# Sums over partitions as two half-width matmuls: diagonal quarters for the head sums, column halves for the sums over all features

## The reference, cut to what matters

```python
def rms_norm(x, gain):
    xf = x.astype(jnp.float32)
    y = xf * lax.rsqrt(jnp.mean(xf * xf, axis=-1, keepdims=True) + EPS)
    return (y * gain.astype(jnp.float32)).astype(x.dtype)
...
h = rms_norm(x, norm_mix[i])                # over all 1024 features, twice a layer
q = rms_norm(qkv[:, :, 0], q_gain)          # over the 64 features of each head
k = rms_norm(qkv[:, :, 1], k_gain)
```

## Time and profile before

| | |
|---|---|
| median of 3 runs | 2962.67 us (2961.53 to 2964.29) |
| the profiled execution | 2964.98 us |
| its span | 2962.8 us |
| TensorE busy (matmuls) | 2815.3 us, 95% of the span |
| TensorE weight loads (beside the matmuls) | 2238.2 us, 76% |
| GpSimd, ACT, DVE busy | 46%, 37%, 34% |
| mean granted TensorE clock | 0.983 |

### The profile page before, as it was taken

One profiled execution on the slowest core, in us unless ns is written; L12 is line 12 of the kernel. 1 busy time (PEld: TensorE's weight loads), 2 busy tenths in 40 slices (PEclk: granted clock), 3 DMA queues, 4 the chain that ended last, 5 costly groups with the idle time before them and its releaser, 6 DMA issues.

```text
span 2962.8 us, 35778 instructions
## 1 busy us (share of the span) xinstructions
PE 2815.3 (95%) x13900; PEld 2238.2 (76%) x13900; DVE 1014.8 (34%) x1906; ACT 1100.3 (37%) x1644; POOL 1370.1 (46%) x1073
## 2 busy tenths in 40 slices
PE   7899899999989999998899998999999899899999
PEld 5876678888756788887677776788887866678887
DVE  3034431113476411225465554311122034431112
ACT  4245442223445422333333433422334245443222
POOL 3466644445464444444243342444445366444443
PEclk9999999999989999999999999999999999999999
DMA  4232123332431232333111110233322232123322
GB/s 120 85 80 57 43 72 100 99 99 85 100 71 44 66 99 92 99 99 93 29 43 43 29 43 29 72 100 100 99 94 84 86 71 60 34 85 100 99 91 79
DMA packets 271749, 227.70 MB, mean 77 GB/s; under 512 B 30100, under 2 KB 259220, under 8 KB 271620
## 3 DMA queue, kind: packets, MB, share of 16 engines
q1 hardware_dynamic: 260880, 216.29, 24.1%
q10 hardware_dynamic: 10740, 9.65, 1.4%
HBM read 223.61 MB, written 2.30 MB: 76 GB/s over the span
## 4 chain that ended last, share of the span: by engine, by line
PE 83%; DVE 7%; POOL 4%; ACT 4%; issue 1%; DMA 0%; ACTq 0%; DVEq 0%; POOLq 0%
PE bank L1756 47%; PE bank L1667 15%; PE bank L1815 5%; POOL w_lo L555 3%; PE bank L2125 2%; PE bank L2137 2%; PE bank L2134 1%; PE bank L1792 1%; PE bank L1710 1%; ACT w_hi L688 1%; POOL arena L577 1%; PE bank L1866 1%; PE bank L1970 1%; PE bank L1998 1%; PE bank L1882 1%
## 5 line engine op out<-in xcount | busy, mean ns | idle before, releaser
L555 POOL TENSOR_TENSOR w_lo<-raw,w_hi 128x512 fp32r<-128x512 f32 x808 | 1068.5, 1355 | 1268.3 <-ACT w_hi L688 1268.3
L688 ACT ACTIVATE w_hi<-raw 128x2048 fp32r<-128x2048 f32 x202 | 385.5, 1908 | 476.6 <-PE bank L1756 423.3
L1756 PE MATMUL bank<-h_hi,w_hi 128*128 128x512 f32 x1024 | 400.8, 391 | 0.0
L1756 PE MATMUL bank<-h_hi,w_lo 128*128 128x512 f32 x1024 | 398.4, 389 | 0.0
L1756 PE MATMUL bank<-h_lo,w_hi 128*128 128x512 f32 x1024 | 398.4, 389 | 0.0
L1756 PE MATMUL bank<-g_hi,w_hi 128*128 128x512 f32 x1024 | 398.3, 389 | 0.0
L1756 PE MATMUL bank<-g_lo,w_hi 128*128 128x512 f32 x1024 | 398.3, 389 | 0.0
L1756 PE MATMUL bank<-g_hi,w_lo 128*128 128x512 f32 x1024 | 398.3, 389 | 0.0
L1667 PE MATMUL bank<-h_hi,w_hi 128*128 128x512 f32 x784 | 331.0, 422 | 6.9 <-POOL w_lo L555 4.6
L1667 PE MATMUL bank<-h_lo,w_hi 128*128 128x512 f32 x784 | 321.1, 410 | 0.0
L1667 PE MATMUL bank<-h_hi,w_lo 128*128 128x512 f32 x784 | 317.9, 406 | 0.0
(11 more groups left out here) (261 smaller groups left out, 3932.7 us busy)
## 6 DMA issues: line engine op xcount, KB each, us to landing
raw<-in_mlp_w SPq DMA_DIRECT2D x128, 1024.0 KB, 5.2
raw<-in_a_w_in SPq DMA_DIRECT2D x48, 512.0 KB, 5.0
raw<-in_c_w_in SPq DMA_DIRECT2D x32, 512.0 KB, 5.2
raw<-in_a_w_in SPq DMA_DIRECT2D x12, 1024.0 KB, 5.0
raw<-in_b_w_in SPq DMA_DIRECT2D x18, 256.0 KB, 4.1
raw<-in_a_w_out SPq DMA_DIRECT2D x4, 1024.0 KB, 4.8
raw<-in_b_w_in SPq DMA_DIRECT2D x4, 1024.0 KB, 5.4
arena<-bias_scratch ACTq DMA_DIRECT2D x16, 256.0 KB, 3.5
```

The costliest lines, as they stand in the source:

```text
L555: ins = nc.gpsimd.tensor_tensor(w_lo[s][:, k, :], raw[s][:, k, :], w_hi[s][:, k, :].bitcast(F32), ALU.subtract)
L688: nc.scalar.activation(w_hi[s][:], raw[s][:], ACT.Copy).then_inc(w_hi_done, 1)
L1756: mm = nc.tensor.matmul(lin_bank[j][:], w[s][:, c, P * j:P * j + P], a[:, c, :], start=c + z == 0, stop=c == CT - 1 and z == 2)
```

## The change

Each of the three sums becomes two matmuls. For sums over all features (`norm`, `square_sum`) the first uses the left 64 columns of `ones` and writes partitions 0 to 63 of the bank, the second the right 64 columns and partitions 64 to 127; both contract over all 128 rows. For the head sums (`sum_qk`) the first uses rows 0 to 63 and columns 0 to 63 of `halves` on partitions 0 to 63 of the squares, the second rows and columns 64 to 127 on the other half, and the zero quarters of `halves` are not used. Where a semaphore is raised it is raised by the second matmul. The waits and everything else stay.

```diff
             def norm(m, columns=False):
 
                 pe.wait_ge(ss_added, ss_before(m) + 7)
-                mm = nc.tensor.matmul(stat_bank[:], ones, ss, start=True, stop=True)
+                for z in (0, HD):
+                    mm = nc.tensor.matmul(stat_bank[z:z + HD, :], ones[:, z:z + HD], ss, start=True, stop=True)
...
             def square_sum(m, c):
 
                 pe.wait_ge(sq_done, 8 * m + c + 1)
-                mm = nc.tensor.matmul(stat_bank[:], ones, sq[c % 2], start=c == 0, stop=c == CT - 1)
+                for z in (0, HD):
+                    mm = nc.tensor.matmul(stat_bank[z:z + HD, :], ones[:, z:z + HD], sq[c % 2], start=c == 0,
+                                          stop=c == CT - 1)
                 mm.then_inc(sq_summed if c < CT - 1 else norm_sum, 1)
...
                 sqs = mem[kind]["sq"]
-                nc.tensor.matmul(stat_bank[:], halves, sqs[Q % len(sqs)], start=True, stop=True).then_inc(ssq_done, 1)
+                for z in (0, HD):
+                    r = slice(z, z + HD)
+                    mm = nc.tensor.matmul(stat_bank[r, :], halves[r, r], sqs[Q % len(sqs)][r, :], start=True, stop=True)
+                mm.then_inc(ssq_done, 1)
```

## The result

The changed kernel takes 2981.4 us (median of 6 runs, 2975.37 to 2987.14) against 2964.44 us (6 runs) of the kernel before: a ratio of 1.0053 with a 95% interval of 1.0042 to 1.0063. It is slower by half a per cent, the forecast's sign and size: 15.7 us, where the ratio gives 15.7 us (12.5 to 18.7). Its profiled execution has a span of 2980.8 us, 18.0 more than the one before.

The account below looks back on a forecast made before the run. TensorE's stream, busy 95% and carrying 83% of the chain, was taken as the bound. Head sums 9.9, squares 3.6 and norms 2.2 us make 15.7, giving 2978.4 us on the median (2980.7 on the profiled execution); range 2968 to 2997.

Parts of the forecast that it names:

- The cost of a visit: Mid-stream on TensorE: 1.32 us from last product to second one after a sum becomes 0.32 + 1.02 + 0.34 = 1.68, +0.36.
- Side by side: Head sums' two diagonal quarters overlap as halves do, leaving only the cost of going in and out; chance 0.70, 2973 to 2986.
- The first rival: Head sums' quarters run in turn: 3012.8 us fully, 2995.6 if only first and last record stand alone; chance 0.13.
- How many are paid: On the chain: 40 of 58 head sums, 6 norms, 10 single squares and 2 pairs; 18 head sums and 2 squares covered.
- The second and third rival: Second, nearly free: head sums add nothing, 2968.5 us, chance 0.11. Third, faster: four records in one record time, 2953.5, chance 0.06.
- a sum behind a wait: Where TensorE waited for the squares: 1.19 us becomes 1.36, +0.17, for 9 head sums and 4 squares.
- Product on both sides: Sums between products on TensorE: 1.32 us becomes 1.68, +0.36, for 19 of the 40 head sums.

Follow-up runs that it names:

- lone quarter: Changed kernel with one layer 0 head sum given only its first quarter: 1.00 us for that quarter, as for a pair; no whole-kernel time is given.
- the head sums alone: Kernel before with only the 58 head sums divided into quarters, sums over all features left whole: 2973.77 us, ratio 1.0032.
- the float32r kernel: Kernel before with the 48 head sums of the two dilated-attention layers as one float32r matmul each: 2942.77 us, ratio 0.9934.

## Why the prediction was right

**The cost of a visit.** The steps 0.32, 1.02 and 0.34 came out as 0.32, 1.00 and 0.34. They were taken from other instructions (row halves of 384 and 512 columns, column halves of 128). Both new forms, 64x64 and 128x64, have the same steps. Between 1.02, taken from a form with 64 columns of weights, and 1.06, from row halves with 128, the former was the right one, so form is not quite without effect.

**Side by side.** The step with the most at stake, 34 us, rested on analogy, as the trace had no quarter. The lone quarter shows it directly. The first rival fell with it. The rule of the Trainium skill that was weighed against the rows (TensorEngine Tiling (Array Packing), Restrictions and Gotchas) says that different row tiles can't access the same PSUM bank at the same time; here they do, in different partitions of bank 7, at 1.00 us for two as for one. The measurement decides for this form; row tiles that write the same partitions were not run.

**How many are paid.** 40 head sums were put on the chain; in the changed kernel 42 of them are pieces of it, with 6 norms, 12 single sums of squares and the 2 pairs. Both squares of layer 0 that were covered before came in, and one head sum more in each attention layer, such as the one at 239.97. These four were not in the sum and may be worth up to 1.4 us. Doubling sums at paid and covered places confirmed the split: 0.87 us each against none.

**The second and third rival.** Covered sums are free, but GpSimd does not set the pace of the attention layers as a whole: the head sums alone cost 9.5 us. No quarter visit was under 1.32 us, and a record of a quarter takes as long as one of the whole array, so nothing could be gained.

**What the sum left out.** The steps sum to 15.6, and the profiled execution grew by 18.0. One term was mis-sized: that a sum behind a wait costs 0.17. At four of the nine such places (60.68, 73.69, 2270.16 and 2283.17 us before) the visit cost nothing. At the first of them, the time from the last product ahead of the sum to the second one behind it was 1.69 us (60.18 to 61.87) and is 1.66 now (61.68 to 63.34). The sum alone grew by 0.15 as forecast, but the division of the sum before had put the products later, and the squares were there when they ended. That is 0.7 us less than forecast. Product on both sides cost 0.34 instead of 0.36, 0.4 us less in all, and the four sums that came in make up to 1.4 us more.

Of the 18.0 us, 3.5 lie in the stretch of layer 2 where the granted clock stayed low for longer. That the ratio gives 15.7 as well is therefore in part luck. Its interval is 12.5 to 18.7, errors of either sign met in the sum, and both profiled executions of the changed kernel have the long stretch, which was not forecast. The six runs spread from 2975 to 2987 us; how much of that is layer 2 is not known, as only profiled executions show it.

## What to carry to other kernels

Price a divided matmul by the distance between its neighbours' starts, not by its own duration: in TensorE's stream of products dividing the array cost 0.34 us each time it was entered and left, with quarters as with column halves, and about 0.15 where divided work followed or where something only waited for the result. A wait ahead of it can swallow it whole. It gives something back only if the parts do different work that the whole array would do one after the other, as the row halves of the earlier trace rows do, four records in the time of two. Keep visits of the same form together, and look first at the number of passes: a sum against ones in full fp32 cost nearly four products, and a float32r one cost one. To say which copies of a repeated instruction matter, walk the chain and count them, then confirm with a doubled instruction at the places on it and off it. And before a difference of a few microseconds is explained, compare how long the granted clock was low in each stage: here that alone moved one stage by 5 us.

## What was not expected

- Added TensorE work in its own waits need not cost anything and may even gain: 18 sums more of 0.86 us each, ratio 0.9985 (0.9977 to 0.9994), with the two attention stages 20.5 us at half the clock instead of 30.7; two more at each of these places gave 0.9995 (0.9986 to 1.0004), and in the float32r kernel 0.9934 became 0.9910.
- Layer 2's mixer took 530.2 to 535.1 us from kernel to kernel, most of it in the last head, with 3.4 or 13.7 us of low clock there, by whether the low clock began a microsecond later or earlier.
- A matmul on one quarter of the array ran ahead of one issued before it on another quarter, so a semaphore on the last matmul can be relied on for the others only if the parts are equally long.
- Leaving 64x64 for 128x64 costs as much as leaving for the whole array (0.52 from the last records), and staying in 128x64 costs nothing (0.42).
